# Modulation products of two bodies in one block, their weights asked for together: a decoder layer on one Trainium2 core

## The chip, the core and the metric

The kernel runs on one core of one Trainium2 chip. The metric is the device time of one execution in microseconds (us). TensorE is called PE in the profile, and its weight loads PEld; VectorE is DVE, ScalarE is ACT, GpSimd is POOL, and SyncE, which issues nearly all transfers, is SP. A transfer is a DMA.

## What is computed

One decoder layer over 256 prompt tokens and 8 x 4 sample tokens, 288 columns in all: a half-step SwiGLU feed-forward, an attention mixer and a second half-step feed-forward. Each sub-layer is modulated by shift, scale and gate, which come from a conditioning vector c of each of 9 sequences. Cut to what matters here:

```python
def adaln_params(c, w_ada, b_ada):
    m = jax.nn.silu(c) @ w_ada + b_ada
    return jnp.split(m[:, None, :], 3 * N_SUBLAYERS, axis=-1)

def run_layer(x, c, mixer, ...):
    sh1, sc1, gt1, sh2, sc2, gt2, sh3, sc3, gt3 = adaln_params(c, w_ada, b_ada)
    x = x + MACARON * gt1 * swiglu(modulate(x, g_ffn1, sh1, sc1), w1_ffn1, w3_ffn1, w2_ffn1)
    heads, state = mixer(modulate(x, g_mix, sh2, sc2))
    x = x + gt2 * (heads @ w_out)
    x = x + MACARON * gt3 * swiglu(modulate(x, g_ffn2, sh3, sc3), w1_ffn2, w3_ffn2, w2_ffn2)
    return x, state
```

The change concerns `silu(c) @ w_ada`, a 2048 x 18432 matrix in float32 for 9 columns of c, called the modulation products here.

## The kernel before, in words

All weights are streamed from HBM once. A **tile** is a 128-column slice of a weight matrix, 1 MB: SP loads it into one of two halves of `raw`, ACT copies it to `w_hi` (rounded), DVE computes `w_lo = raw - w_hi`, each in two halves, and PE makes three products per 128 rows (`products`, lines 714 to 723). Two tiles make a **body** (`pair`, line 742): tile a into bank `acc_a`, tile b into `acc_b`. Bodies are strung into segments (`plan`, lines 99 to 130): the first feed-forward has three chunks, each an "up" segment (w1 and w3, followed by Silu and a product) and a "down" segment (w2, added to x).

Of the modulation weights the first 32 slices (shift and scale of the first feed-forward) are needed at once. They go through a ring of three buffers, `adax`, in the first segment: eight steps in which PE alternates groups of modulation products (`ada_group`, line 664) with `first_step` (line 672). The other 112 slices are spread over the 56 bodies of the segments marked `ada`: 12 up, 8 down, 14 up, 8 down and 14 up bodies. Each such body has, ahead of its two tiles, one **block** of modulation products (`ada_body`, line 736, and `ada_slots`, line 635) out of the one buffer `adaw` (2 slices, 2 MB). A slice holds half of the input rows for 256 output columns, so two blocks, an even and an odd one, make one **group** of four output columns of 128. They accumulate in one bank; then DVE turns the bank and adds the bias (`ada_finish`, line 1480), in the second body of the group. There are 28 such groups.

What sets the order around it:

- SP issues in program order (`stream`, line 489). In an ada body it asks for tile a, waits until PE has used the present block, asks for the two slices of the next, and asks for tile b. A tile's request waits until `w_lo` of the tile two before it has been made (`slot`, line 461).
- ACT, after the first segment, runs `split_high(segs[1], 0, 0)`, then `first_silu(0)` and `first_silu(1)`, then `split_high(segs[1], 1, 0)` (lines 1173 to 1177). The first tile of the next segment on PE waits for `acc_a_read`, which `first_silu(0)` raises (lines 745 and 746).
- POOL starts its loads of the attention constants (`big`, 1.5 MB), and then 64 loads of 4 KB (`lfc`), when `h_ready` has reached 8 (line 597). DVE raises `h_ready` with the eighth `h_lo` (line 1517). Later POOL stores `rev` and spreads it over HBM (`rev_dram`, line 609).
- The buffers `hf` and `sq` (normalisation) lie unused between the first segment and the squares of the last down segment.

Of the kernel before, what the change touches and what calls it, by code (L numbers as in the profile page):

```python
# [30 lines left out]
F32 = mybir.dt.float32  # L31
# [6 lines left out]
P = 128  # L38
D = 2048
KT = D // P  # L40
HEADS, HD = 8, 128
TP, NB, NS = 256, 8, 4
TS = NB * NS
T = TP + TS
# [3 lines left out]
ADA = NPAR * KT  # L48
# [8 lines left out]
SQR, SQL = KT // 4, 4  # L57
# [4 lines left out]
STEPS0, FIRST = 8, 3  # L62
GROUP = 4
# [13 lines left out]
REV = 383  # L77
# [152 lines left out]
def decoder_layer(nc, xT, cT, gT, bada, nwT, bfg, relb, pt, cst, cst2, ohrev, addrev, selh,  # L230
# [9 lines left out]
    with ExitStack() as ctx:  # L240
        top = [16512]

        def at(name, shape, dt, off):
            return nc.alloc_sbuf_tensor_at(name, shape, dt, offset=off)

        def sb(name, shape, dt=F32):
            n = int(np.prod(shape[1:])) * 4
            t = at(name, shape, dt, top[0])
            top[0] += -(-n // 32) * 32
            return t  # L250

        def sem(name):
            return ctx.enter_context(nc.semaphore(name))
# [22 lines left out]
        mix0 = top[0]  # L276

        g_hi, g_lo = sb("g_hi", [P, 15, T], F32R), sb("g_lo", [P, 15, T], F32R)
        adaw = sb("adaw", [P, 2, KT * P])
# [5 lines left out]
        sq0 = top[0] - 2 * SQL * T * 4 - 2 * TS * 4  # L285
# [8 lines left out]
        assert 2 * P + 2 * NC <= 2 * KT * NC  # L294

        y0, ms, tt = (at(n, [P, T], F32, sq0 + k * T * 4) for k, n in enumerate(("y0", "ms", "tt")))
        rev = at("rev", [HEADS, REV], F32, sq0 + 3 * T * 4)

        adax = at("adax", [P, ADAX, 2, KT * P], F32, mix0)
        assert 2 * ADAX * KT * P * 4 <= 2 * 15 * T * 4 + 2 * KT * P * 4  # L300
# [7 lines left out]
        vn0 = top[0]  # L308
        v_new = sb("v_new", [TS, HEADS * HD])
        lfr0 = top[0]  # L310
        lfr = sb("lfr", [P, PAGES, P])
        ohr = at("ohr", [32, REV], F32, vn0 + 4096)
        adr = at("adr", [HEADS, REV], F32, vn0 + 5632)

        fa_sb, fe = at("fa_sb", [HEADS, T], F32, vn0), at("fe", [HEADS, T], F32, vn0 + T * 4)

        z = at("z", [P, 6 * HEADS, T], F32, mix0)
        hf0 = mix0 + 6 * HEADS * T * 4
        assert hf0 <= top[0]
        yh = at("yh", [P, 2, T], F32, hf0)  # L320
# [34 lines left out]
        def kv(m, j):  # L355
# [16 lines left out]
        ss2 = pairs[2]  # L372


        names = """ld_small ld_x w_landed0 w_landed1 hi_ready lo_ready w_used acc_a_read acc_b_read ada_landed
            adax_landed0 adax_landed1 adax_landed2 ada_used ada_turned ada_fin first_done
            c_ready sq_ready sq_used y0_ready hf_ready hhi_ready hn_ready gain_ready h_ready g_ready
            act_chain dve_chain y_stored heads_stored v_stored ss_read ld_att ld_rel ld_selw ld_pages
# [4 lines left out]
        S = {n: sem(n) for n in names.split()}  # L383
# [3 lines left out]
        def run(seg, eng, body, first=0, chain=None, per=0):  # L387

            if first >= seg.bodies:
                return  # L390
            with eng.Fori(first, seg.bodies) as i:
                if chain:
                    chain.loop(i, first, per)
                body(i)
            if chain:
                chain.end(seg.bodies)
# [10 lines left out]
        def tile_no(b, j):  # L407

            return 2 * b + j + (2 * b >= FA_TILE)
# [19 lines left out]
        def _(sp):  # L429
# [31 lines left out]
            def slot(seg, j, i):  # L461

                n, r = seg.n0 + j, (seg.n0 + j) % 2
                if not (isinstance(i, int) and n + 2 * i < 2):

                    sp.wait_ge(S["lo_ready"], 2 * (n - 1) + 4 * i)
                src = WS[seg.src]
                if seg.kind == "up":
                    ap = src[bass.ds(2 * (seg.ff0 + i) + j, 1), :, :]
                elif seg.kind == "down":  # L470
                    ap = src[bass.ds(seg.d0 + 2 * i + j, 1), :, seg.k0 * P:(seg.k0 + seg.nk) * P]
                else:
                    b = j // 2 if j < FA_TILE else (j - 1) // 2
                    row = 0 if j == FA_TILE else 1 + PAIR_Z[b] + (j - tile_no(b, 0))
                    ap = src[row:row + 1, :, :]
                sp.dma_start(raw[:, r, 0:seg.nk * P], ap.rearrange("a p n -> p (a n)"))\
                  .then_inc(S[f"w_landed{r}"], 16)

            def ada_pair(seg, i, odd, group):

                if isinstance(i, int) and seg.pair0 + i == 0:
                    sp.wait_ge(S["ada_used"], 2 * STEPS0)
                else:
                    sp.wait_ge(S["ada_used"], 2 * STEPS0 + seg.pair0 + i)
                for j in range(2):
                    sp.dma_start(adaw[:, j, :], w_ada[bass.ds(2 * KT + 2 * seg.pair0 + GROUP * group + 2 * j + odd, 1), :, :]
                                 .rearrange("a p n -> p (a n)")).then_inc(S["ada_landed"], 16)

            def stream(some, first=0):
                for seg in some:  # L490
                    if seg.ada:
                        for i in range(2):
                            slot(seg, 0, i)
                            ada_pair(seg, i, i, 0)
                            slot(seg, 1, i)
                        with sp.Fori(1, seg.bodies // 2) as i:
                            for odd in range(2):
                                slot(seg, 0, 2 * i + odd)
                                ada_pair(seg, 2 * i + odd, odd, i)
                                slot(seg, 1, 2 * i + odd)  # L500
                        continue

                    def body(i, seg=seg):
                        slot(seg, 0, i)
                        slot(seg, 1, i)
                    if seg.norm is not None:
                        body(0)
                        for j in range(2):
                            sp.wait_ge(S["shift_sum"], 2 + j + 1)
                            slot(seg, j, 1)  # L510
                    run(seg, sp, body, 2 if seg.norm is not None else first)

            stream(ffn1[1:])

            def load_half(m):
# [62 lines left out]
            sp.wait_ge(S["p_o"], 2 * HEADS)  # L578
            sp.dma_start(x[:, 7:KT, :], x_dram[:, 7:KT, :]).then_inc(S["x_back"], 16)
            stream([out], 1)  # L580
            stream(segs[segs.index(out) + 1:])

            last, k = segs[-1], KT - 2
# [50 lines left out]
        def _(pe):  # L634
            def ada_slots(w, half):

                cols = w.rearrange("p a (k t j n) -> p a k t j n", k=HALF, t=2, j=4)
                for k in range(HALF):
                    kt = HALF * half + k
                    for j in range(4):  # L640
                        last = pe.matmul(ada_part[32 * j:32 * j + 32, 0:P], sc32[:, kt, :], cols[:, :, k, :, j, :],  # L641
                                         start=kt == 0, stop=kt == KT - 1, tile_position=(0, 32 * j))
                last.then_inc(S["ada_used"], 1)
# [81 lines left out]
            def tile(seg, j, i, bank, mid=None):  # L725
                n, r = seg.n0 + j, (seg.n0 + j) % 2
                m_hi, m_lo = (h_hi, h_lo) if seg.moving == "h" else (g_hi, g_lo)
                late = seg.up0 if seg.moving == "g" else None
                half = KT // 2
                for q, (a, b) in enumerate(((0, half), (half, seg.nk))):  # L730
                    pe.wait_ge(S["lo_ready"], 2 * n + q + 1 + 4 * i)
                    products(bank, r, m_hi, m_lo, a, b, seg.nk, late).then_inc(S["w_used"], 1)
                    if q == 0 and mid:
                        mid()

            def ada_body(seg, i, odd, group):
                if not odd:
                    pe.wait_ge(S["ada_turned"], group)
                pe.wait_ge(S["ada_landed"], 32 * (seg.pair0 + 1) + 32 * i)
                ada_slots(adaw[:, :, :], odd)  # L740

            def pair(seg, i, mid_b=None, ada=None):
                if seg.ada:
                    ada_body(seg, i, *ada)
                early = seg is segs[1] and isinstance(i, int) and i == 0
                pe.wait_ge(S["acc_a_read"], 1 if early else seg.ra + i)
                tile(seg, 0, i, acc_a)
                pe.wait_ge(S["acc_b_read"], 1 if early else seg.rb + i)
                tile(seg, 1, i, acc_b, mid_b)

            def ada_pairs(seg):
                g = 2 * KT // GROUP + seg.pair0 // 2
                for i in range(2):
                    pair(seg, i, None, (i, g))
                with pe.Fori(1, seg.bodies // 2) as i:
                    pair(seg, 2 * i, None, (0, i + g))
                    pair(seg, 2 * i + 1, None, (1, i + g))

            def shift_products(seg, r, j):

# [229 lines left out]
            for b in range(2, PAIRS):  # L990
                if 2 * b == FA_TILE:
                    tile(mix, FA_TILE, 0, bank[2])
                for j in range(2):
                    pe.wait_ge(S["acc_b_read" if j else "acc_a_read"], (mix.rb if j else mix.ra) + b)
                    n = mix.n0 + tile_no(b, j)
# [1017 lines left out]
```

## Time and profile before

| | before |
|---|---|
| median of 3 runs | 2530.42 us (2529.33 to 2534.91) |
| the profiled execution, its own time | 2532.02 us |
| its span, first to last instruction | 2530.4 us |
| mean granted clock of TensorE | 0.991 of full speed |
| PE busy, of the span | 2444.4 us (97%) |
| DVE, ACT, POOL busy | 1190.1, 910.4, 45.1 us |
| bytes moved, mean rate | 619.52 MB, 245 GB/s |
| modulation products of the 56 ada bodies | 3584 records, 109.4 us busy |

A PE record is longer than the step to the next one, since matrix products are pipelined; so costs are read from starts, not from durations. Float32 products leave two records each, so a block of 32 products shows 64. The span is shorter than the time of its execution by 1.6 us, which lies around it.

### The profile page before, as it was taken

The page shows a single profiled execution, that of the slowest core. Times are in us where ns is not written, and L with a number is a line of the kernel's source. Part 1 is how long each engine was busy: PE and PEld are TensorE (multiplying, and loading weights), DVE is VectorE, ACT ScalarE, POOL GpSimd, SP SyncE. Part 2 cuts the span into 40 slices and gives each one's busy share as a digit, 9 for nine tenths or more (in the row PEclk, how much of TensorE's full clock was granted, in tenths as well). Part 3 has the DMA queues.
Part 4 walks back from the last instruction along what each step waited for, and adds up shares of the span by engine and source line. Part 5 has one row for each costly group of instructions (what it writes and reads, how often), then busy time and mean ns, then how long its engine had stood idle before and what let it go on. Part 6 is the DMA issues. An engine that isn't in the chain of part 4 may idle for free.

```text
span 2530.4 us, 57187 instructions
## 1 busy us (share of the span) xinstructions
PE 2444.4 (97%) x23159; PEld 2326.6 (92%) x23159; DVE 1190.1 (47%) x1903; ACT 910.4 (36%) x1134; POOL 45.1 (2%) x87
## 2 busy tenths in 40 slices
PE   4899999999999999999999998999999999999999
PEld 4899999999999999999788765998999999999999
DVE  2344444344444446774344434566445444454444
ACT  2332322332223334664244323455333333333332
POOL 0032000000000000000000000000000000000000
PEclk8999999999999999999999999999999999999999
DMA  8988777777887764558899998444444444454444
GB/s 326 395 318 302 284 291 289 293 276 276 300 302 285 282 235 152 211 189 316 313 330 345 360 353 323 173 164 150 166 163 157 171 165 163 158 170 166 165 166 153
DMA packets 140007, 619.52 MB, mean 245 GB/s; under 512 B 17896, under 2 KB 24320, under 8 KB 90736
## 3 DMA queue, kind: packets, MB, share of 16 engines
q1 hardware_dynamic: 135792, 608.54, 65.8%
q0 software_dynamic: 4096, 9.27, 1.0%
q8 instruction: 90, 1.47, 0.2%
q14 instruction: 29, 0.24, 0.0%
HBM read 608.29 MB, written 11.03 MB: 245 GB/s over the span
## 4 chain that ended last, share of the span: by engine, by line
PE 86%; DMA 7%; DVE 2%; SPq 2%; ACT 2%; issue 1%; DVEq 0%; ACTq 0%
PE banks L720 25%; PE banks L721 25%; PE banks L722 24%; PE banks L641 5%; DMA adax<-in_w_ada_dram 2%; DMA raw<-in_w_in_dram 2%; PE banks L909 1%; PE banks L913 1%; SPq L546 1%; DMA kv_y<-in_winv_dram 1%; PE banks L851 1%; DVE w_lo L1385 1%; DMA adaw<-in_w_ada_dram 1%; DMA kv_b<-in_wink_dram 1%; PE banks L688 0%
## 5 line engine op out<-in xcount | busy, mean ns | idle before, releaser
L720 PE MATMUL banks<-h_hi,w_hi 128*128 128x288 f32 x3664 | 1088.5, 297 | 14.1 <-DVE w_lo L1385 9.5
L721 PE MATMUL banks<-h_lo,w_hi 128*128 128x288 f32 x3664 | 1081.9, 295 | 0.0
L722 PE MATMUL banks<-h_hi,w_lo 128*128 128x288 f32 x3664 | 1080.9, 295 | 0.0
L1385 DVE TENSOR_TENSOR w_lo<-raw,w_hi 128x1024 fp32r<-128x1024 f32 (+2 forms) x670 | 764.3, 1182 | 591.0 <-ACT w_hi L1087 589.6
L1087 ACT ACTIVATE w_hi<-raw 128x1024 fp32r<-128x1024 f32 (+2 forms) x670 | 672.1, 1025 | 924.3 <-PE banks L722 521.6
L720 PEld LDWEIGHTS banks<-h_hi,w_hi 128*128 128x128 f32 x3664 | 689.9, 188 | 40.2 <-issue 31.3
L721 PEld LDWEIGHTS banks<-h_lo,w_hi 128*128 128x128 f32 x3664 | 689.9, 188 | 0.6
L722 PEld LDWEIGHTS banks<-h_hi,w_lo 128*128 128x128 f32 x3664 | 689.7, 188 | 0.0
L720 PE MATMUL banks<-g_hi,w_hi 128*128 128x288 f32 x1376 | 409.1, 297 | 0.1
L721 PE MATMUL banks<-g_lo,w_hi 128*128 128x288 f32 x1376 | 406.6, 295 | 0.0
L722 PE MATMUL banks<-g_hi,w_lo 128*128 128x288 f32 x1376 | 406.4, 295 | 0.0
L720 PEld LDWEIGHTS banks<-g_hi,w_hi 128*128 128x128 f32 x1376 | 259.4, 188 | 4.3 <-issue 3.2
L721 PEld LDWEIGHTS banks<-g_lo,w_hi 128*128 128x128 f32 x1376 | 259.5, 189 | 0.0
L722 PEld LDWEIGHTS banks<-g_hi,w_lo 128*128 128x128 f32 x1376 | 259.5, 189 | 0.0
L1194 ACT ACTIVATE su<-banks 128x288 f32<-128x288 f32 x83 | 34.1, 411 | 512.2 <-PE banks L722 510.6
L1563 DVE TENSOR_TENSOR tmps<-banks,par 128x32 f32<-128x32 f32 x112 | 21.4, 191 | 272.8 <-PE banks L722 272.8
L1580 DVE TENSOR_TENSOR gf<-su,banks 128x288 f32<-128x288 f32 x86 | 39.1, 454 | 204.8 <-PE banks L722 203.1
L641 PE MATMUL banks<-adaw,sc 128*32 128x128 f32 x3584 | 109.4, 274 | 1.8 <-DMA adaw<-in_w_ada_dram 1.8
L641 PEld LDWEIGHTS banks<-adaw,sc 128*32 128x32 f32 x3584 | 94.4, 110 | 11.1 <-issue 9.0
L641 PE MATMUL banks<-adax,sc 128*32 128x128 f32 x1024 | 38.4, 315 | 36.1 <-DMA adax<-in_w_ada_dram 35.9
L641 PEld LDWEIGHTS banks<-adax,sc 128*32 128x32 f32 x1024 | 33.5, 127 | 39.9 <-issue 24.0
L1567 DVE SCALAR_TENSOR_TENSOR x<-banks,par,x 128x256 f32 (+1 forms) x112 | 54.2, 484 | 16.1 <-DVE x L1566 15.5
(250 smaller groups left out, 1198.2 us busy)
## 6 DMA issues: line engine op xcount, KB each, us to landing
raw<-in_w_dram SPq DMA_DIRECT2D x166, 1024.0 KB, 4.8
adaw<-in_w_ada_dram SPq DMA_DIRECT2D x112, 1024.0 KB, 6.7
raw<-in_w_dram SPq DMA_DIRECT2D x64, 896.0 KB, 4.5
raw<-in_w_in_dram SPq DMA_DIRECT2D x49, 1024.0 KB, 8.0
adax<-in_w_ada_dram SPq DMA_DIRECT2D x32, 1024.0 KB, 12.7
raw<-in_w_dram SPq DMA_DIRECT2D x32, 960.0 KB, 4.7
raw<-in_w_out_dram SPq DMA_DIRECT2D x16, 1024.0 KB, 5.0
kv_a<-in_vpool_dram SPq DMA_DIRECT2D x36, 256.0 KB, 4.9
```

The source lines that it names most:

```text
L546: sp.dma_start(kv(m, j), src.rearrange("a p n -> p (a n)")).then_inc(S[f"kv_landed{HOME[m]}"], 16)
L641: last = pe.matmul(ada_part[32 * j:32 * j + 32, 0:P], sc32[:, kt, :], cols[:, :, k, :, j, :], start=kt == 0, stop=kt == KT - 1, tile_posit ...
L720: pe.matmul(bank[:, 0:T], hi, m_hi[:, k, :], start=k == 0, stop=False)
L721: pe.matmul(bank[:, 0:T], hi, m_lo[:, k, :], start=False, stop=False)
L722: last = pe.matmul(bank[:, 0:T], lo, m_hi[:, k, :], start=False, stop=k == nk - 1)
L851: return pe.transpose(dst, src, ident[0:src.shape[0], 0:src.shape[0]])
L909: last = pe.matmul(main[32 * j:32 * j + 32, p // 4, (p % 4) * P:(p % 4 + 1) * P], qbd[j // 2][:, j % 2, 32 * h:32 * h + 32], kv(m, j)[:, i ...
L1087: act.activation(w_hi[:, r, a:b], raw[:, r, a:b], ACT.Copy).then_inc(S["hi_ready"], 1)
L1194: act.activation(su[:, :], (scaled_banks[0] if scaled else acc_a)[:, 0:T], ACT.Silu).then_inc(S["acc_a_read"], 1)
L1385: dve.tensor_tensor(w_lo[:, r, a:b], raw[:, r, a:b], w_hi[:, r, a:b].bitcast(F32), ALU.subtract).then_inc(S["lo_ready"], 1)
L1567: dve.scalar_tensor_tensor(xp, bank[:, 0:TP], par[:, bass.ds(gate * NC, 1)], xp, ALU.mult, ALU.add).then_inc(S["acc_b_read" if j else "acc ...
L1580: dve.tensor_tensor(gf[:, :], su[:, :], b[:, 0:T], ALU.mult).then_inc(S["acc_b_read"], 1)
```

## The change

The modulation products of two bodies stand in one block ahead of the first of them. A second buffer, `ada2`, lies where `hf` and the start of `sq` are. The four slices of a group are asked for together, after the whole present group has been multiplied and after the requests for the four tiles of its two bodies. Each buffer has its own landing semaphore. For the first group SP waits until `h_ready` has reached 8 (so that `hf` is free) and asks for its four slices ahead of the first tile. `rev` moves to another place.

```diff
-        rev = at("rev", [HEADS, REV], F32, sq0 + 3 * T * 4)
...
+        rev = at("rev", [HEADS, REV], F32, vn0)
...
+        ada2 = at("ada2", [P, 2, KT * P], F32, mix0 + 6 * HEADS * T * 4)
...
-            def ada_pair(seg, i, odd, group):
-
-                if isinstance(i, int) and seg.pair0 + i == 0:
-                    sp.wait_ge(S["ada_used"], 2 * STEPS0)
-                else:
-                    sp.wait_ge(S["ada_used"], 2 * STEPS0 + seg.pair0 + i)
-                for j in range(2):
-                    sp.dma_start(adaw[:, j, :], w_ada[bass.ds(2 * KT + 2 * seg.pair0 + GROUP * group + 2 * j + odd, 1), :, :]
-                                 .rearrange("a p n -> p (a n)")).then_inc(S["ada_landed"], 16)
+            def ada_halves(seg, group, used):
+                sp.wait_ge(S["ada_used"], used)
+                for odd in range(2):
+                    for j in range(2):
+                        t = 2 * KT + 2 * seg.pair0 + GROUP * group + 2 * j + odd
+                        sp.dma_start((ada2 if odd else adaw)[:, j, :], w_ada[bass.ds(t, 1), :, :]
+                                     .rearrange("a p n -> p (a n)")).then_inc(S[f"ada_landed{odd}"], 16)
+
+            def ada_bodies(seg, k, more=True):
+                for i in range(2):
+                    slot(seg, 0, 2 * k + i)
+                    slot(seg, 1, 2 * k + i)
+                if more:
+                    ada_halves(seg, k + 1, 2 * STEPS0 + seg.pair0 + 2 * (k + 1))
...
                     if seg.ada:
-                        for i in range(2):
-                            slot(seg, 0, i)
-                            ada_pair(seg, i, i, 0)
-                            slot(seg, 1, i)
-                        with sp.Fori(1, seg.bodies // 2) as i:
-                            for odd in range(2):
-                                slot(seg, 0, 2 * i + odd)
-                                ada_pair(seg, 2 * i + odd, odd, i)
-                                slot(seg, 1, 2 * i + odd)
+                        last = 2 * (seg.pair0 + seg.bodies) == ADA - 2 * KT
+                        if seg.pair0 == 0:
+                            sp.wait_ge(S["h_ready"], STEPS0)
+                            ada_halves(seg, 0, 2 * STEPS0)
+                        ada_bodies(seg, 0)
+                        with sp.Fori(1, seg.bodies // 2 - last) as k:
+                            ada_bodies(seg, k)
+                        if last:
+                            ada_bodies(seg, seg.bodies // 2 - 1, False)
                         continue
...
-            def ada_body(seg, i, odd, group):
-                if not odd:
-                    pe.wait_ge(S["ada_turned"], group)
-                pe.wait_ge(S["ada_landed"], 32 * (seg.pair0 + 1) + 32 * i)
-                ada_slots(adaw[:, :, :], odd)
+            def ada_group_of(group):
+
+                pe.wait_ge(S["ada_turned"], group)
+                for odd in range(2):
+                    pe.wait_ge(S[f"ada_landed{odd}"], 32 * (group - 2 * KT // GROUP + 1))
+                    ada_slots((ada2 if odd else adaw)[:, :, :], odd)
 
             def pair(seg, i, mid_b=None, ada=None):
-                if seg.ada:
-                    ada_body(seg, i, *ada)
+                if ada is not None:
+                    ada_group_of(ada)
...
                 for i in range(2):
-                    pair(seg, i, None, (i, g))
+                    pair(seg, i, None, None if i else g)
                 with pe.Fori(1, seg.bodies // 2) as i:
-                    pair(seg, 2 * i, None, (0, i + g))
-                    pair(seg, 2 * i + 1, None, (1, i + g))
+                    pair(seg, 2 * i, None, i + g)
+                    pair(seg, 2 * i + 1)
```

## Rows read from the trace of the kernel before

**Rows 1.** The page: the span, and the modulation products of the 56 ada bodies.

```profile
span 2530.4 us, 57187 instructions
...
L641 PE MATMUL banks<-adaw,sc 128*32 128x128 f32 x3584 | 109.4, 274 | 1.8 <-DMA adaw<-in_w_ada_dram 1.8
```

**Rows 2.** Timeline of PE (start us, us, engine line op, out<-in, count): the first ada bodies.

```profile
130.75 1.96 PE L641 MATMUL banks<-adaw,sc 128*32 128x128 f32 x64
...
132.64 0.40 PE L720 MATMUL banks<-h_hi,w_hi 128*128 128x288 f32 x1
...
145.53 1.95 PE L641 MATMUL banks<-adaw,sc 128*32 128x128 f32 x64
...
160.31 1.95 PE L641 MATMUL banks<-adaw,sc 128*32 128x128 f32 x64
```

**Rows 3.** Timeline of ACT in the second feed-forward: Silu of two bodies without modulation products.

```profile
2011.11 0.41 ACT L1194 ACTIVATE su<-banks 128x288 f32<-128x288 f32 x1 [5.36 <-PE banks L722]
...
2023.80 0.41 ACT L1194 ACTIVATE su<-banks 128x288 f32<-128x288 f32 x1 [5.37 <-PE banks L722]
```

**Rows 4.** Timeline of PE in the first segment: two blocks on end.

```profile
94.07 3.70 PE L641 MATMUL banks<-adax,sc 128*32 128x128 f32 x128
```

**Rows 5.** Timeline of all engines, end of the first segment, in order of time.

```profile
115.00 0.33 SPq L476 DMA_DIRECT2D raw<-in_w_dram  x1
...
120.53 1.28 SPq L486 DMA_DIRECT2D adaw<-in_w_ada_dram  x2
...
123.48 0.75 DVE L1517 TENSOR_TENSOR h_lo<-hf,h_hi 128x576 fp32r<-128x576 f32 x1
...
123.59 6.38 SPq L476 DMA_DIRECT2D raw<-in_w_dram  x2
...
124.53 0.56 POOL L598 DMA_DIRECT2D big<-in_cst_dram  x1 [120.89 <-DVE h_lo L1517]
```

**Rows 6.** DMA issues by line: operation, count, KB each, median us to landing.

```profile
raw<-in_w_dram SPq DMA_DIRECT2D x166, 1024.0 KB, 4.8
...
rev_dram<-rev_rows POOLq DMA_DIRECT2D x1, 1532.0 KB, 21.0
big<-in_cst_dram POOLq DMA_DIRECT2D x1, 1506.0 KB, 10.1
```

**Rows 7.** Stretches: us, busy (instructions) of PE, PEld, DVE, ACT, POOL; clock, DMA, GB/s.

```profile
115.00:120.00 5.00, 2.43 (x60) 2.43 (x64) 0.76 (x1) 0.83 (x2) 0.00 (x0) 0.84 1.03 382
125.00:130.00 5.00, 5.00 (x41) 5.00 (x39) 2.44 (x3) 3.70 (x4) 3.10 (x7) 1.00 1.02 426
130.00:135.00 5.00, 5.00 (x89) 4.63 (x87) 3.24 (x7) 2.38 (x4) 1.66 (x4) 1.00 1.00 417
135.00:140.00 5.00, 5.00 (x40) 5.00 (x39) 2.62 (x5) 1.04 (x4) 1.60 (x3) 1.00 1.01 375
140.00:145.00 5.00, 5.00 (x40) 5.00 (x39) 2.36 (x2) 1.60 (x2) 2.00 (x4) 1.00 0.95 357
```

**Rows 8.** Timeline of ACT after the first segment.

```profile
126.16 2.01 ACT L1087 ACTIVATE w_hi<-raw 128x1024 fp32r<-128x1024 f32 x2 [3.01 <-PE banks L690]
128.19 1.28 ACT L1171 ACT_TABLE_LOAD   x1
129.48 0.41 ACT L1171 ACTIVATE su<-banks 128x288 f32<-128x288 f32 x1
```

**Rows 9.** Timeline of PE: work resumed after a wait in the first segment.

```profile
117.57 2.92 PE L641 MATMUL banks<-adax,sc 128*32 128x128 f32 x64 [3.70 <-DMA adax<-in_w_ada_dram]
120.42 0.61 PE L688 MATMUL banks<-h_hi,w_hi 128*128 128x288 f32 x1
...
121.79 0.31 PE L690 MATMUL banks<-h_hi,w_lo 128*128 128x288 f32 x1
```

**Rows 10.** Timeline of PE: the one block of an ada body that came late.

```profile
250.89 1.95 PE L641 MATMUL banks<-adaw,sc 128*32 128x128 f32 x64 [1.83 <-DMA adaw<-in_w_ada_dram]
```

**Rows 11.** Timeline of POOL: the spreading of rev over HBM.

```profile
229.65 1.10 POOL L609 DMA_DIRECT2D rev_dram<-rev_rows  x1 [5.45 <-DMA rev_rows<-rev]
```

More of the change, by code:

```diff
@@ L317, in decoder_layer @@
         z = at("z", [P, 6 * HEADS, T], F32, mix0)
+        ada2 = at("ada2", [P, 2, KT * P], F32, mix0 + 6 * HEADS * T * 4)
+        assert 2 * KT * P * 4 <= 2 * 2 * SQL * T * 4
         hf0 = mix0 + 6 * HEADS * T * 4
@@ L372, in decoder_layer @@
         ss2 = pairs[2]
-        names = """ld_small ld_x w_landed0 w_landed1 hi_ready lo_ready w_used acc_a_read acc_b_read ada_landed
+        names = """ld_small ld_x w_landed0 w_landed1 hi_ready lo_ready w_used acc_a_read acc_b_read ada_landed0 ada_landed1
             adax_landed0 adax_landed1 adax_landed2 ada_used ada_turned ada_fin first_done
```

## The prediction

> **What bounds the kernel now.** I read the page first: the modulation products of the ada bodies waited for their weights for 1.8 us in all [rows 1]. Their 3584 records are 56 blocks of 64. The timeline of PE shows what they cost: a body starts every 14.78 us, from 130.75 to 145.53 to 160.31 [rows 2], with nothing idle between. So PE sets the time of this stretch, and only PE's own steps, or a new wait of PE, can change it. The rest of the kernel runs the same instructions in the same order and moves with the end of this stretch.
>
> **The gain in the steady state.** Two Silu starts of bodies without modulation products are 12.69 us apart [rows 3], so a block standing alone costs 14.78 - 12.69 = 2.09 us of PE's time. In the first segment two blocks stand on end: 128 records in 3.70 us, where 64 take 1.96 [rows 4, 2], so the second costs 1.74 us. The difference, 0.35 us, is the cost of changing from full-width products to 32-column ones and back. The change saves one such turn in each of 28 groups. In the first group it is lost in a wait (below), which leaves 27 x 0.35 = 9.4 us. In rows 4 the wait between the two blocks is against a constant, in the new loop against a register; the trace has no such pair. Bounds: nothing saved, or 9.4. I take 9.4: at mid-tile such waits stand between products, and the 12.69 us leave no room for a cost there.
>
> **The late block.** One block came 1.83 us late [rows 10], while POOL spread 1.5 MB over HBM, from 229.65 for 21 us [rows 11, 6]. In the change the group that follows begins near 160.31 + 14.4 (the delay found below) + 3 x 29.2 = 262, and its weights are asked for at the end of the block before, near 237. POOL's transfer ends at 250.7; at half the rate until then and the full rate after it, weights that need 12.5 us alone (next part) are in by 256. Bounds 0 to 1.8 gained; I take 1.8.
>
> **The steady transfers.** Per group 4 MB of modulation weights and 4 MB of tiles move, as before. Now the 4 MB are asked for at the end of the block, behind the last tile's request. 1 MB lands 4.8 us after its request [rows 6] and further ones follow every 1.0486/0.4 = 2.6 us, at 400 GB/s, between the 357 and 426 of [rows 7]. So they land 4.8 + 3 x 2.6 = 12.5 us on, and are wanted after four tiles, 2 x 12.69 = 25.4 us on. The request queued behind them on SP, tile a of the next group, lands some 2.6 us later, 15 us on; its tile is multiplied 29 us on, with 2.0 us of rounding [rows 8] and DVE's differences between. Cost nothing, with some 10 us in hand. If that cover went, PE would wait for `w_lo`. DVE turns the bank in the second body as before, after both blocks are long done. In the second body no block lies between the tiles any more, but the second feed-forward runs so, at an even 12.69 us.
>
> **The start of the stretch.** Here the change costs. Before, SP asks for the first tile at 115.00 and for the first block's slices at 120.53, while the first segment still runs [rows 5]. Now SP waits for the eighth `h_lo`, made at 123.48 + 0.75 = 124.23 [rows 5], and then asks for 4 MB of modulation weights ahead of that tile. POOL starts its 1.5 MB on the same event, at 124.53 [rows 5, 6]. Nothing asked for earlier covers the gap.
>
> The tile is the fifth MB of the queue: 5 x 1.0486 + 1.54 (POOL) = 6.79 MB. From a request at 124.35 the full rate counts from 124.35 + 4.8 - 2.6 = 126.6. At the rates of the same stretches before, 426 to 130, 417 to 135, 375 to 140 and 357 after [rows 7], 1.45 + 2.08 + 1.88 MB have moved by 140, and the last 1.38 MB take 3.9 us: the tile lands at 143.9. The two blocks, whose slices come before it, are done in this wait.
>
> PE doesn't start then. Its first tile waits for `acc_a_read`, which `first_silu(0)` raises, and in ACT's program that stands behind the rounding of this very tile. Rounding, table load and Silu go from 126.16 to 129.89 in the trace [rows 8], 3.73 us. So PE starts at 143.9 + 3.7 = 147.6, where it started at 132.64 [rows 2]. Two bodies without a block between them and the turn to the next block follow: 12.69 + (145.53 - 132.64) = 25.6, so the second group's block starts at 173.2 in place of 160.31: 12.9 us lost.
>
> On top comes the clock. After a wait of 3.70 us the next block took 2.92 us in place of 1.96, and the stretch's mean granted clock was 0.84 [rows 9, 7]: part of it at 1.2 of 2.4 GHz. The block lost 0.96 us, and the five steps from 120.42 to 121.79 took 1.37 us in place of 5 x 0.132 (a tile's 48 products in 12.69/2): 0.7 more, so about 1.7. PE now waits three times in a row, for the first half, the second half and the tile, and only what is left of the fall after the last counts. Bounds 0 to 3.4 us (twice that); I take 1.5, since part of the fall may be spent inside the waits. Start in all: 14.4 us lost.
>
> Bounds of the start: if POOL's bytes cost nothing and all goes at 426 GB/s, the tile lands at 138.9, and the loss is 7.9 us without a fall of the clock; at 357 GB/s throughout it lands at 145.6, and with 3.4 us of clock the loss is 18.0.
>
> The row's 426 and 417 GB/s speak against a rule. The Trainium skill, "DMA: Bandwidth & Descriptors", section Specifications, gives an HBM limit of about 358 GB/s for one core; by it the tile would land at 126.6 + 6.79/0.358 = 145.6 and the sum below would be 1.7 us higher. Rows 7 show 426 and 417 GB/s with the queue full, so this case's trace decides, though its last stretch fell to 357.
>
> **The sum.** +14.4 (start) - 9.4 (turns) - 1.8 (late block) = +3.2 us. Against the profiled execution's 2532.02 us that is 2535.2; that execution lies 1.6 above the median of the runs, 2530.42, so the forecast for the median is 2533.6. A measurement of this kernel tells about 0.2%, 5.1 us, from no change. So the forecast is a change of 0.13% that can't be told apart.
>
> **The rivals.**
> (1) Slower: the start is longer. Place: the first tile behind 4 MB and POOL's. Price: at 357 GB/s throughout 1.7 us, and at a clock that stays low twice as long 1.9 more, so 2533.6 + 3.6 = 2537.2. The rate alone gives 2535.3. It decides from a landing at 145.8, or a start loss above 16.3 us. For it: the fall to 357 at the end of rows 7. Against it: there the queue had run short. The rate alone is also what the Trainium skill's limit in "DMA: Bandwidth & Descriptors" would make of the start, and the trace bears it out in its last stretch only.
> (2) Slower: the joint isn't free. A register wait between the blocks costs as much as a turn: 9.4 us not saved, 2543.0. It decides from 0.07 us for a joint (1.9/27). Against it: rows 2 show even blocks, with two waits ahead, and odd ones, with one, at the same 14.78.
> (3) Slower: tiles come late, or the change doesn't join the blocks, since the second half's slices land after the first half is used. At 0.5 us for a group that is 14 us: 2547. Against it: the 10 us in hand.
> (4) Faster: the start costs its lower bound, 7.9, and the rest is as in the sum: 2527.1, which can't be told apart either; beyond -5.1 a gain unseen in the rows is needed.
>
> **How the numbers follow.** Forecast 0.55, with rival 1 near its decision point another 0.22, rival 2 0.08, rival 3 0.05, rival 4 0.10, of which half beyond 0.2%. Of rival 1, 0.04 is the rate alone and stays inside the bound. So same 0.55 + 0.04 + 0.05 = 0.64, slower 0.18 + 0.08 + 0.05 = 0.31, faster 0.05. The range goes from 2528.5, a little above the lower bound of all terms, to 2541.0, which takes in rival 1 and half of rival 2. Left out are the rest of 2, rival 3 and the far side of 4, less than 0.2.
>
> **What would show it.** Right: blocks of 128 records of about 3.7 us, 29.2 us apart with up bodies (29.56 before); the first product of the first ada body near 147.6 and its cause Silu; the second group's block near 174; no PE wait for `adaw` near 250; the end of the ada stretch 3 us later. Wrong: group starts still 29.5 us apart (rival 2), PE waits for `w_lo` within the stretch (rival 3), or a first tile landing before 140 (rival 4) or after 145.8 (rival 1).

## The result, and the profile after

The changed kernel takes 2538.72 us (median of 14 runs, 2532.69 to 2543.78) against 2533.05 us before (14 runs, 2528.17 to 2537.17). The ratio is 1.0023, 95% interval [1.0014, 1.0032]: it is slower, by about 5.7 us. It lies inside the range of the prediction. The change is 2.5 us more than the +3.2 us forecast; the time lies 5.1 us above the forecast 2533.6, because the kernel before came out 2.6 us higher as well than in its first three runs. The 0.23% are just past the 0.2% from which a change was said to be told from none.

The page shows what PE now waited for. The modulation products stand on two lines, one for each buffer; before, they had waited 1.8 us [rows 1], now it is 5.6 and 3.1.

```profile
span 2538.4 us, 57119 instructions
...
L648 PE MATMUL banks<-adaw,sc 128*32 128x128 f32 x1792 | 56.4, 279 | 5.6 <-DMA adaw<-in_w_ada_dram 5.6
...
L648 PE MATMUL banks<-ada,sc 128*32 128x128 f32 x1792 | 55.8, 278 | 3.1 <-DMA ada<-in_w_ada_dram 3.1
```

The timeline of PE in the changed kernel shows where: both waits are in the first group, and a third one, for Silu, stands between them and the first tile.

```profile
135.54 3.64 PE L648 MATMUL banks<-adaw,sc 128*32 128x128 f32 x64 [5.61 <-DMA adaw<-in_w_ada_dram]
142.31 3.64 PE L648 MATMUL banks<-ada,sc 128*32 128x128 f32 x64 [3.13 <-DMA ada<-in_w_ada_dram]
148.74 0.61 PE L727 MATMUL banks<-h_hi,w_hi 128*128 128x288 f32 x1 [2.80 <-ACT su L1179]
...
176.71 1.95 PE L648 MATMUL banks<-adaw,sc 128*32 128x128 f32 x64
...
205.93 1.95 PE L648 MATMUL banks<-adaw,sc 128*32 128x128 f32 x64
207.70 0.51 PE L648 MATMUL banks<-ada,sc 128*32 128x128 f32 x12
...
264.37 1.95 PE L648 MATMUL banks<-adaw,sc 128*32 128x128 f32 x64
...
918.60 1.96 PE L648 MATMUL banks<-adaw,sc 128*32 128x128 f32 x64
```

The last group in the timeline of PE in the kernel before:

```profile
912.82 1.95 PE L641 MATMUL banks<-adaw,sc 128*32 128x128 f32 x64
```

Three readings. The first tile begins at 148.74, where it was 132.64, and the second group's block at 176.71 in place of 160.31 [rows 2]: 16.4 us lost. From there a group takes 205.93 - 176.71 = 29.22 us in place of 2 x 14.78 = 29.56: 0.34 us saved each time, and the second half follows the first within 1.77 us. And the block near 250, which had come 1.83 us late [rows 10], does so no more (264.37 is three even steps after 176.71). The last group starts at 918.60, before at 912.82: 5.8 us later, which is 16.4 - 26 x 0.34 - 1.83 = 5.7. The two medians, 5.7 us apart, fit a rest of the kernel that carries this to its end. The two traces alone would not show it: their spans differ by 8.0 us, since what follows the start of the last group takes 1619.8 us here and 1617.6 before. In the other eight traces of this case it takes 1610.6 to 1619.0 us, so the 2.2 us between these two lie in that spread.

The timelines of SP and of ACT show the chain of the start. SP begins to ask when `h_ready` lets it, and ACT gets the first tile only at 144.97; rounding, table load and Silu follow as in [rows 8].

```profile
124.39 0.80 SPq L486 DMA_DIRECT2D adaw<-in_w_ada_dram  x2
125.23 1.19 SPq L486 DMA_DIRECT2D ada<-in_w_ada_dram  x2
126.46 28.06 SPq L478 DMA_DIRECT2D raw<-in_w_dram  x4
```

```profile
144.97 2.00 ACT L1095 ACTIVATE w_hi<-raw 128x1024 fp32r<-128x1024 f32 x2 [21.40 <-DMA raw<-in_w_dram]
146.99 1.28 ACT L1179 ACT_TABLE_LOAD   x1
148.28 0.41 ACT L1179 ACTIVATE su<-banks 128x288 f32<-128x288 f32 x1
```

The stretches of the same time, with columns as in [rows 7]: PE is idle from 130 to 135, the granted clock falls to 0.50, 1.2 of 2.4 GHz, and the stretch from 150 still has a mean of 0.59; so it is back only towards the end of that one.

```profile
125.00:130.00 5.00, 4.92 (x38) 4.69 (x36) 0.10 (x1) 0.00 (x0) 3.11 (x7) 1.00 0.88 344
130.00:135.00 5.00, 0.00 (x0) 0.00 (x0) 0.00 (x0) 0.00 (x0) 1.78 (x4) 0.86 0.98 416
135.00:140.00 5.00, 3.64 (x64) 3.22 (x64) 0.00 (x0) 0.00 (x0) 1.60 (x3) 0.50 1.02 378
140.00:145.00 5.00, 2.69 (x52) 2.50 (x56) 0.00 (x0) 0.04 (x1) 1.88 (x4) 0.50 1.02 396
145.00:150.00 5.00, 2.20 (x25) 1.72 (x18) 3.57 (x5) 3.66 (x4) 1.86 (x4) 0.50 0.30 63
150.00:155.00 5.00, 5.00 (x26) 5.00 (x25) 4.32 (x9) 2.60 (x4) 1.60 (x3) 0.59 0.52 201
```

### The profile page after: what moved, and what is told of

Read it like the earlier page. It is cut to its first block, busy times and chain, and to the rows that moved or that the text cites. A ratio compares the mean times of both kernels' runs of the same rounds, so it can differ in the third digit from the quotient of the medians.

```text
span 2538.4 us, 57119 instructions
## 1 busy us (share of the span) xinstructions
PE 2443.4 (96%) x23159; PEld 2332.4 (92%) x23159; DVE 1190.1 (47%) x1903; ACT 910.0 (36%) x1134; POOL 45.0 (2%) x87
## 4 chain that ended last, share of the span: by engine, by line
PE 85%; DMA 7%; DVE 3%; SPq 2%; ACT 2%; issue 1%; DVEq 0%; ACTq 0%
PE banks L727 25%; PE banks L728 24%; PE banks L729 24%; PE banks L648 5%; DMA raw<-in_w_in_dram 2%; SPq L553 2%; DMA adax<-in_w_ada_dram 2%; PE banks L917 1%; DMA raw<-in_w_dram 1%; PE banks L921 1%; DMA kv_e<-in_wink_dram 1%; DVE w_lo L1393 1%; PE banks L859 1%; ACT w_hi L1095 1%; DMA kv_w<-in_winv_dram 0%
## 5 line engine op out<-in xcount | busy, mean ns | idle before, releaser
L648 PE MATMUL banks<-adaw,sc 128*32 128x128 f32 x1792 | 56.4, 279 | 5.6 <-DMA adaw<-in_w_ada_dram 5.6
L648 PE MATMUL banks<-ada,sc 128*32 128x128 f32 x1792 | 55.8, 278 | 3.1 <-DMA ada<-in_w_ada_dram 3.1
## 6 DMA issues: line engine op xcount, KB each, us to landing
adax<-in_w_ada_dram SPq DMA_DIRECT2D x32, 1024.0 KB, 12.7
```

## The experiments

The theory: all of the loss lies in the start, and each joint saves 0.34 us. Its rivals: that the joined requests lengthen the stretch, and that the saving comes from the second buffer or from asking earlier, not from the joint. The kernels are edits of the changed kernel, timed against the kernel before on the same chip.

**The first group put back.** The first group's blocks stand apart, and its requests go out as early as before; the other 27 groups stay joined.

```diff
...
-                            sp.wait_ge(S["h_ready"], STEPS0)
-                            ada_halves(seg, 0, 2 * STEPS0)
-                        ada_bodies(seg, 0)
+                            slot(seg, 0, 0)
+                            sp.wait_ge(S["ada_used"], 2 * STEPS0)
+                            ada_half(seg, 0, 0)
+                            slot(seg, 1, 0)
+                            slot(seg, 0, 1)
+                            sp.wait_ge(S["h_ready"], STEPS0)
+                            ada_half(seg, 0, 1)
+                            slot(seg, 1, 1)
+                            sp.wait_ge(S["ada_used"], 2 * STEPS0 + 1)
+                            ada_half(seg, 1, 0)
+                            sp.wait_ge(S["ada_used"], 2 * STEPS0 + 2)
+                            ada_half(seg, 1, 1)
+                        else:
+                            ada_bodies(seg, 0)
...
-                    pair(seg, i, None, None if i else g)
+                    pair(seg, i, None, (g, (i,)) if apart else None if i else (g,))
```

> The changed kernel, with the first group alone put back: its two blocks stand ahead of their own bodies, its first tile and first slices are asked for as early as before, and the second group's weights are asked for half by half. The other 27 groups stay joined. Theory (the loss is all in the start, the joints save 0.34 us each): the first tile's products begin at 132.6 us as before, the second group's block near 160.3, groups 29.22 us apart, no late block near 250; 11 us less than the kernel before, ratio 0.9957. Rival (the joined requests lengthen the stretch or what follows it): not below the kernel before, ratio 1.000 to 1.002.

Measured: 2518.68 us against 2531.33, ratio 0.9956 [0.994, 0.9971]. Its timeline of PE:

```profile
131.04 1.95 PE L665 MATMUL banks<-adaw,sc 128*32 128x128 f32 x64
...
132.92 0.40 PE L744 MATMUL banks<-h_hi,w_hi 128*128 128x288 f32 x1
...
160.60 1.95 PE L665 MATMUL banks<-adaw,sc 128*32 128x128 f32 x64
...
248.26 1.96 PE L665 MATMUL banks<-adaw,sc 128*32 128x128 f32 x64
250.03 1.93 PE L665 MATMUL banks<-ada,sc 128*32 128x128 f32 x64
...
902.48 1.96 PE L665 MATMUL banks<-adaw,sc 128*32 128x128 f32 x64
```

The start is where it was before, and from 160.60 to 248.26 lie three groups of 29.22 us without a wait. From the first block to the last group's it is 902.48 - 131.04 = 771.4 us, before 912.82 - 130.75 = 782.1; these 10.6 us and the last group's own 0.34 are the 11 expected, and the rest of the 12.7 us between the medians lies in the spread of the runs. So the loss was the start, and what remains is a gain. By its ratio to the kernel before, this version beats both kernels.

**The same again**, on another chip, beside the kernel with two buffers below.

> The kernel of e1_first_apart once more, beside the one with two buffers on the same chip. Theory: groups 29.22 us apart, ratio 0.9957, 9 us below the kernel with two buffers and apart from it in the interval. Rival (the gain seen before was one chip's or chance): ratio above 0.998.

Measured: 2522.31 us against 2531.05, ratio 0.9967 [0.9954, 0.998]; groups 29.22 us apart. The expected 0.9957 lies in both intervals. The kernel with two buffers, on this chip, has [0.9982, 1.0001], which doesn't touch this one's. The distance of the medians is 2529.06 - 2522.31 = 6.8 us for the expected 9. The traces have the expected size: from the first block to the last group's it is 900.90 - 129.46 = 771.4 us here and 911.30 - 131.13 = 780.2 with two buffers, 8.7 apart, and the last group's own 0.34 comes on top.

**Two buffers without the joint.** Each block ahead of its own body, its weights asked for a body further ahead; the start as before.

```diff
...
-                for i in range(2):
-                    slot(seg, 0, 2 * k + i)
-                    slot(seg, 1, 2 * k + i)
-                if more:
-                    ada_halves(seg, k + 1, 2 * STEPS0 + seg.pair0 + 2 * (k + 1))
+                for odd in range(2):
+                    slot(seg, 0, 2 * k + odd)
+                    if more or not odd:
+                        sp.wait_ge(S["ada_used"], 2 * STEPS0 + seg.pair0 + 2 * k + odd)
+                        ada_half(seg, k + odd, 1 - odd)
+                    slot(seg, 1, 2 * k + odd)
...
-                    pair(seg, 2 * i, None, i + g)
-                    pair(seg, 2 * i + 1)
+                    pair(seg, 2 * i, None, (i + g, (0,)))
+                    pair(seg, 2 * i + 1, None, (i + g, (1,)))
```

> The kernel before with the second buffer alone: each block ahead of its own body, the weights of a block asked for one body further ahead, into the buffer that the block before last has left; the start as before. Theory (the joint saves, not the second buffer or the earlier request): groups 29.56 us apart as before, no late block near 250, second group's block near 160.3; 1.8 us below the kernel before, ratio 0.9993. Rival (it was the earlier request or the second buffer that shortened the groups): 29.22 us apart, ratio 0.9957.

Measured: 2529.06 us against 2531.05, ratio 0.9992 [0.9982, 1.0001]. The timeline of PE:

```profile
160.69 1.96 PE L664 MATMUL banks<-adaw,sc 128*32 128x128 f32 x64
...
190.25 1.96 PE L664 MATMUL banks<-adaw,sc 128*32 128x128 f32 x64
...
219.81 1.96 PE L664 MATMUL banks<-adaw,sc 128*32 128x128 f32 x64
...
249.37 1.95 PE L664 MATMUL banks<-adaw,sc 128*32 128x128 f32 x64
```

The steps are 29.56 us, as before, and the late block is gone. So asking earlier buys the late block alone, and the 0.34 us a group are the joint's.

**The blocks apart, the requests joined.** PE's side alone was undone, in all groups; SP's was left.

```diff
...
-                    pair(seg, i, None, None if i else g)
+                    pair(seg, i, None, (g, (i,)))
...
-                    pair(seg, 2 * i, None, i + g)
-                    pair(seg, 2 * i + 1)
+                    pair(seg, 2 * i, None, (i + g, (0,)))
+                    pair(seg, 2 * i + 1, None, (i + g, (1,)))
```

> The changed kernel with its requests as they are, but each block ahead of its own body again. Theory: groups 29.56 us apart, so 27 x 0.34 = 9 us given back, and the second block of the first group no longer falls into the wait, 2 us more; start loss as in the changed kernel; some 17 us above the kernel before, ratio 1.0066. Rival (the joint is worth nothing, the changed spacing comes from the requests): like the changed kernel, ratio 1.002.

Measured: 2682.22 us against 2531.33, ratio 1.0604 [1.0587, 1.0621]: neither. The timelines of SP, of ACT and of PE around one group of this kernel:

```profile
237.03 0.85 SPq L486 DMA_DIRECT2D adaw<-in_w_ada_dram  x2
238.08 1.03 SPq L486 DMA_DIRECT2D ada<-in_w_ada_dram  x2
239.75 21.55 SPq L478 DMA_DIRECT2D raw<-in_w_dram  x4
```

```profile
253.54 2.00 ACT L1096 ACTIVATE w_hi<-raw 128x1024 fp32r<-128x1024 f32 x2 [9.65 <-DMA raw<-in_w_dram]
```

```profile
249.63 1.95 PE L648 MATMUL banks<-adaw,sc 128*32 128x128 f32 x64
255.91 0.61 PE L727 MATMUL banks<-h_hi,w_hi 128*128 128x288 f32 x1 [4.32 <-DVE w_lo L1394]
```

Both expectations had left out when the 4 MB are asked for. They wait for the odd block, which now ends in the middle of the group, one body ahead of the next group's block in place of two. The next tile stands behind them in the queue and lands at 253.54, 16.5 us after their request at 237.03 (14.8 in each of the next two groups). PE wants it at 255.91 - 4.32 = 251.59, 14.6 us after the request, and it has still to be rounded and split: 4.32 us of waiting here, 91.7 us in 27 such waits from 160 to 1100 by the table of waits. After 24 of the 27 the granted clock falls as well: its mean in the 5 us from the first product on is 0.50 to 0.70. The run doesn't price the turn, which the two kernels above do; it shows what the cover is that the prediction counted on. The timelines of SP and of PE in the changed kernel, for the group at the same place:

```profile
240.05 0.85 SPq L486 DMA_DIRECT2D adaw<-in_w_ada_dram  x2
...
249.57 19.40 SPq L478 DMA_DIRECT2D raw<-in_w_dram  x4
```

```profile
268.00 0.40 PE L727 MATMUL banks<-h_hi,w_hi 128*128 128x288 f32 x1
```

There the tile is wanted 28 us after the request of the 4 MB. It is asked for only 9.5 us after them, when its half of `raw` is free, and PE doesn't wait for it.

**Asking for the first tile and the first half early**, all groups joined:

```diff
...
-                            sp.wait_ge(S["h_ready"], STEPS0)
-                            ada_halves(seg, 0, 2 * STEPS0)
-                        ada_bodies(seg, 0)
+                            slot(seg, 0, 0)
+                            sp.wait_ge(S["ada_used"], 2 * STEPS0)
+                            ada_half(seg, 0, 0)
+                            sp.wait_ge(S["h_ready"], STEPS0)
+                            ada_half(seg, 0, 1)
+                            slot(seg, 1, 0)
+                            slot(seg, 0, 1)
+                            slot(seg, 1, 1)
+                            ada_halves(seg, 1, 2 * STEPS0 + 2)
+                        else:
+                            ada_bodies(seg, 0)
```

> The changed kernel, all groups joined, but the first tile and the first half's slices are asked for ahead of the wait for h_ready (near 115 and 120 us); the second half's slices after it. Theory: the first block starts at 130.75, the second waits for its slices until about 138.5, the first tile starts near 140.5 to 141, the second group's block near 166 to 167 (160.3 before, 176.7 in the changed kernel); 4 to 5 us below the kernel before, ratio 0.998. Rival (the start is not what costs): as the changed kernel, ratio 1.002.

Measured: 2527.40 us against 2531.33, ratio 0.9988 [0.9976, 0.9999]; the rival's 1.002 lies outside.

```profile
129.79 1.95 PE L662 MATMUL banks<-adaw,sc 128*32 128x128 f32 x64
138.17 3.64 PE L662 MATMUL banks<-ada,sc 128*32 128x128 f32 x64 [6.42 <-DMA ada<-in_w_ada_dram]
141.74 0.61 PE L741 MATMUL banks<-h_hi,w_hi 128*128 128x288 f32 x1
...
168.18 1.95 PE L662 MATMUL banks<-adaw,sc 128*32 128x128 f32 x64
```

The second half lands when expected, at 138.17; its block then runs at the low clock (3.64 us), so the first tile starts at 141.74 and the second group's block at 168.18, 1.2 us later than the latest expected. Two of the three waits are gone, and so is half of the loss.

**POOL's loads begun later**, when the first group has been multiplied:

```diff
-            pool.wait_ge(S["h_ready"], STEPS0)
+            pool.wait_ge(S["ada_used"], 2 * STEPS0 + 2)
```

> The changed kernel, with POOL's loads begun only when the first group has been multiplied. Theory (POOL's 1.5 MB stands in the queue's way): the first tile lands 4 to 5 us sooner, near 140, its products start near 144, the second group's block near 172 in place of 176.7; 0 to 1 us above the kernel before, ratio 1.0003. Rival (transfers don't slow each other, the latency is in the queue alone): as the changed kernel, ratio 1.002.

Measured: 2532.38 us against 2532.10, ratio 1.0005 [0.9995, 1.0015]; the rival's 1.002 lies outside. Timelines of ACT and of PE:

```profile
142.09 2.00 ACT L1095 ACTIVATE w_hi<-raw 128x1024 fp32r<-128x1024 f32 x2 [17.38 <-DMA raw<-in_w_dram]
```

```profile
145.87 0.40 PE L727 MATMUL banks<-h_hi,w_hi 128*128 128x288 f32 x1 [2.68 <-ACT su L1179]
```

SP could ask only at 125.81 in this execution, 1.4 us later than in the changed kernel's; from that request to the tile it is 16.3 us, where it had been 144.97 - 124.39 = 20.6. Three other executions with POOL's loads beside the queue (blocks apart, Silu first, PE kept busy) have 20.2 to 20.4 us. So POOL's loads, 1.5 MB and the first of the small ones, cost the start 3.9 to 4.3 us. The second group's block starts at 172.99.

**Silu first**, ahead of the rounding of the first tile:

```diff
-            split_high(segs[1], 0, 0)
             first_silu(0)
+            split_high(segs[1], 0, 0)
             first_silu(1)
```

> The changed kernel, with ACT's first Silu ahead of the rounding of the first tile. Theory (Silu ends the wait): from the tile's landing to its first product 2.3 us (rounding and difference of one half) in place of 3.8, so 1.5 us sooner, ratio 1.0016. Rival (the difference w_lo ends it anyway): no sooner, ratio 1.002.

Measured: 2536.32 us against 2532.10, ratio 1.0020 [1.0008, 1.0031], an interval that holds both expectations, so the time doesn't decide. The timelines of ACT and PE do:

```profile
144.74 2.00 ACT L1095 ACTIVATE w_hi<-raw 128x1024 fp32r<-128x1024 f32 x2 [16.00 <-DMA raw<-in_w_dram]
```

```profile
147.20 0.58 PE L727 MATMUL banks<-h_hi,w_hi 128*128 128x288 f32 x1 [1.53 <-DVE w_lo L1393]
```

From the tile to its first product it is 2.46 us in place of 148.74 - 144.97 = 3.77, and the wait now ends with `w_lo`. Silu was the last in the chain, worth 1.3 us.

**PE kept busy** in the three waits, with 62 products into an unused bank:

```diff
+            def filler(n):
+                for _ in range(n):
+                    pe.matmul(ssb[:, 0:T], h_hi[:, 0, 0:P], h_hi[:, 1, :], start=True, stop=True)
...
+                    if isinstance(group, int) and group == 2 * KT // GROUP:
+                        if odd == 0:
+                            pe.wait_ge(S["rev_ready"], 1)
+                        filler(26 if odd == 0 else 16)
                     pe.wait_ge(S[f"ada_landed{odd}"], 32 * (group - 2 * KT // GROUP + 1))
                     ada_slots((ada2 if odd else adaw)[:, :, :], odd)
+                if isinstance(group, int) and group == 2 * KT // GROUP:
+                    filler(20)
```

> The changed kernel, with PE multiplying the modulated input by itself into an unused bank (62 products of 288 columns) while it waits for the first group's two halves and the first tile. Theory (the clock fell in those waits and cost 2 to 3 us after them): granted clock 1.00 from 130 to 155, the step between products 0.13 from the first tile on, second group's block near 174.3; ratio 1.0012. Rival (the clock plays no part, the first bodies wait for their tiles): as the changed kernel, 176.7 and ratio 1.002.

Measured: 2535.57 us against 2532.10, ratio 1.0012 [1.0001, 1.0024]: as expected, but the rival's 1.002 lies in the interval too, so the trace has to decide. The stretches, then the timeline of PE:

```profile
135.00:140.00 5.00, 3.94 (x67) 3.55 (x68) 0.00 (x0) 0.00 (x0) 1.61 (x3) 0.66 1.02 379
...
145.00:150.00 5.00, 3.49 (x26) 3.26 (x26) 3.58 (x5) 3.55 (x5) 1.71 (x4) 1.00 0.31 76
150.00:155.00 5.00, 5.00 (x40) 5.00 (x39) 4.63 (x8) 2.34 (x4) 1.61 (x3) 1.00 0.53 193
```

```profile
148.37 0.40 PE L727 MATMUL banks<-h_hi,w_hi 128*128 128x288 f32 x1 [1.51 <-ACT su L1189]
...
173.95 1.96 PE L648 MATMUL banks<-adaw,sc 128*32 128x128 f32 x64
```

The clock still dipped once, from 135 to 140, but was full when the tile came. The two bodies take 173.95 - 148.37 = 25.6 us, exactly the prediction's 12.69 + 12.89, where the changed kernel's took 176.71 - 148.74 = 28.0. So the clock cost 2.4 us.

## Why the prediction held, point by point

- **The turns** (9.4 us): right. 0.34 us a group, 27 x 0.34 = 9.2. That the register wait between the two blocks costs nothing, which no row of before could show, is shown by the 29.22 us and by the 1.77 us between the two halves. Rival 2 falls.
- **The late block** (1.8 us): right; in three kernels with earlier requests it is gone.
- **The steady transfers** (nothing): right for the changed kernel, whose only waits for weights stand in the first group. The margin was smaller than forecast: the prediction has the next tile land 15 us after the 4 MB are asked for, with some 10 us in hand. For the tile wanted at 268.00 ACT's wait ended at 259.79, 19.7 us on, and `w_lo` was made by 263.24, which leaves some 5 us in hand. That the cover is needed, and that PE would wait for `w_lo` without it, is shown by the kernel with blocks apart and requests joined. Rival 3 falls for the change, and names the danger of its neighbour.
- **The start** (14.4 us): the mechanism was right in each link, the size 2.0 us short; it measured 16.4. The first tile came at 144.97, forecast 143.9, which is 1.1. The clock cost 2.4 us, where I took 1.5 inside bounds of 0 to 3.4, which is 0.9. In the clock's term the step that was mis-sized is "since part of the fall may be spent inside the waits": the waits followed one another so closely that the clock was still low at the first tile and stayed so into the stretch from 150. In the landing's term it is not the rate: the stretches from 125 to 145 had 344, 416, 378 and 396 GB/s, 7.7 MB in all, where the forecast counted 6.79 up to the landing. By the trace's queues SP's had moved 5.27 MB by 143, as much as the five MB up to the tile, and the tile landed 2 us after that. So what was too short is the time allowed beside the rate, 4.8 - 2.6 = 2.2 us; the runs don't part it further.
- **The other landing**: the Trainium skill, "DMA: Bandwidth & Descriptors", section Specifications, gives an HBM limit of about 358 GB/s for one core, and by it the tile would have landed at 145.6. That is 0.6 us past the measured 144.97, nearer than my 143.9, but by luck: three of the four stretches ran at 416, 378 and 396 GB/s, above the limit.
- **The sum**: +3.2 us forecast, +5.7 measured, by 16.4 - 9.2 - 1.8 = +5.4. The likeliest case, no change that can be told, did not come: the interval lies above 1, and +5.7 is half a microsecond past the 5.1 that were to be told. What came is next to rival 1, a longer start (forecast 2537.2, +6.8): its start loss above 16.3 us was met by 0.1. The landing and the clock each gave about half of it, and the lower rate that the rival names did not come.

## What to carry to other kernels

A change that saves a little in every round of a loop should be read at its first round too: there the requests have no earlier round to hide behind, and here that cost more than 27 rounds gave. Left out of the first round, the same change is worth 0.3 to 0.4%. And where several loads are asked for together, count what stands behind them in the same queue, from the moment of the request to the moment of its use: 28 us were enough here, 15 cost 6%.

## What the runs showed of the hardware that was not expected

Changing between full-width products and 32-column ones costs PE 0.34 us a turn, without any wait: 2.09 us for a block alone, 1.74 for one on end. And POOL's loads, asked for at the same moment as 5 MB on SP's queue, put the last of these back by 3.9 to 4.3 us, somewhat more than the 1.54/0.417 = 3.7 us that the bytes of the large one take at the rate of [rows 7]. The small loads may be the rest, which no run parts: from 135 to 140 POOL's queue moved 0.02 MB in the changed kernel, and its 244 packets took 10.3% of the DMA engines' time.
